# Two-branch mixer: the columns of w_in multiplied in pairs by seven half-size products

## What is computed

```
h = rmsnorm(x, g);  p = h @ w_in                       # 1024 x 9216
hc, b, c, z_a, q, k, v, z_r, g_a, g_r = split(p)
u = c * hc;  conv = w0*u[t-2] + w1*u[t-1] + w2*u[t]
a = ((b * conv) * silu(z_a)) @ w_a                     # 1024 x 1024
o, state = retention(rotary(q), rotary(k), v, state)   # 4 heads, chunks, per-head decay
r = (head_norm(o) * silu(z_r)) @ w_r                   # 1024 x 1024
x = x + (sigmoid(g_a) * a + sigmoid(g_r) * r) @ w_o    # 1024 x 1024
```

## Time and profile before

| | |
|---|---|
| time, median of 3 runs | 2542.15 us (2541.31 to 2542.98) |
| the profiled execution's span | 2539.6 us, 2.55 us under the median |
| PE busy | 2486.1 us of the span |
| POOL, DVE, ACT busy | 932.1, 857.9, 336.1 us |
| granted clock, mean | 0.991 |

### The profile page before, as it was taken

One profiled execution on the slowest core, in us unless ns is written; L12 is line 12 of the kernel. 1 busy time (PEld: TensorE's weight loads), 2 busy tenths in 40 slices (PEclk: granted clock), 3 DMA queues, 4 the chain that ended last, 5 costly groups with the idle time before them and its releaser, 6 DMA issues.

```text
span 2539.6 us, 35522 instructions
## 1 busy us (share of the span) xinstructions
PE 2486.1 (98%) x15141; PEld 2458.1 (97%) x15141; DVE 857.9 (34%) x805; ACT 336.1 (13%) x469; POOL 932.1 (37%) x426
## 2 busy tenths in 40 slices
PE   7999999999999999999989999999999999999998
PEld 6899999999999999999979999999999999999998
DVE  6552534331222222114384443523222222210153
ACT  5111121100010010001132111111000010000010
POOL 4333333343333333443362333333433333343442
PEclk8999999999999999999989999999999999999999
DMA  5111111111111111115311111111111111111162
GB/s 203 36 44 35 44 40 41 37 42 50 42 45 46 41 41 50 33 53 120 103 53 41 42 41 41 40 34 45 42 46 46 41 43 48 41 33 50 50 121 78
DMA packets 206120, 134.90 MB, mean 53 GB/s; under 512 B 12560, under 2 KB 197104, under 8 KB 204016
## 3 DMA queue, kind: packets, MB, share of 16 engines
q1 hardware_dynamic: 201312, 130.34, 17.9%
q10 hardware_dynamic: 4752, 3.75, 0.5%
HBM read 118.54 MB, written 15.53 MB: 53 GB/s over the span
## 4 chain that ended last, share of the span: by engine, by line
PE 84%; issue 6%; DVE 5%; POOL 2%; ACT 1%; DMA 0%; DVEq 0%; ACTq 0%; POOLq 0%; SPq 0%
PE ps L1044 80%; DVE x L786 1%; DVE act_lo L820 1%; POOL power L419 1%; POOL w_lo L410 1%; POOL w_hi L408 1%; DVE rstds L802 1%; PE ps L1117 1%; PE ps L1124 1%; PE ps L1090 1%; DVE T L764 0%; DVE V L804 0%; ACT row_squares L480 0%; DVE qT L766 0%; PE ps L1223 0%
## 5 line engine op out<-in xcount | busy, mean ns | idle before, releaser
L408 POOL TENSOR_TENSOR w_hi<-w_raw,zero 128x1024 fp32r<-128x1024 f32 x192 | 370.8, 1931 | 1420.0 <-PE ps L1044 1380.9
L1044 PE MATMUL ps<-act_hi,w_hi 128*128 128x364 f32 (+1 forms) x3840 | 858.9, 331 | 25.3 <-DVE act_lo L897 17.9
L1044 PE MATMUL ps<-act_lo,w_hi 128*128 128x364 f32 (+1 forms) x3840 | 848.3, 329 | 0.0
L1044 PE MATMUL ps<-act_hi,w_lo 128*128 128x364 f32 (+1 forms) x3840 | 844.1, 328 | 0.0
L1044 PEld LDWEIGHTS ps<-act_hi,w_hi 128*128 128x128 f32 x3840 | 661.8, 189 | 32.3 <-DVE act_lo L897 19.1
L1044 PEld LDWEIGHTS ps<-act_lo,w_hi 128*128 128x128 f32 x3840 | 666.6, 189 | 0.0
L1044 PEld LDWEIGHTS ps<-act_hi,w_lo 128*128 128x128 f32 x3840 | 665.8, 189 | 0.0
L410 POOL TENSOR_TENSOR w_lo<-w_raw,w_hi 128x1024 fp32r<-128x1024 f32 x192 | 512.5, 2669 | 15.1
L955 DVE TENSOR_TENSOR U<-ps,T 128x1092 f32<-128x1092 f32 x16 | 20.7, 1294 | 278.8 <-PE ps L1044 278.8
L924 DVE TENSOR_TENSOR U<-ps,T 128x728 f32<-128x728 f32 x16 | 14.7, 917 | 258.0 <-PE ps L1044 258.0
L1044 PE MATMUL ps<-o_hi,w_hi 128*128 128x364 f32 (+1 forms) x384 | 85.9, 332 | 5.9 <-DVE r L749 5.9
(11 more groups left out here) (179 smaller groups left out, 1748.2 us busy)
## 6 DMA issues: line engine op xcount, KB each, us to landing
w_raw<-in_w_in_dram SPq DMA_DIRECT2D x144, 512.0 KB, 3.6
x_keep<-x SPq DMA_DIRECT2D x8, 1092.0 KB, 8.4
x<-x_keep SPq DMA_DIRECT2D x8, 1092.0 KB, 7.3
w_raw<-in_w_r_dram SPq DMA_DIRECT2D x16, 512.0 KB, 3.9
w_raw<-in_w_a_dram SPq DMA_DIRECT2D x16, 512.0 KB, 4.6
w_raw<-in_w_o_dram SPq DMA_DIRECT2D x16, 512.0 KB, 4.0
x_rows<-in_x_prompt_dram SPq DMA_DIRECT2D x8, 512.0 KB, 7.0
out_dram<-y_rows SPq DMA_DIRECT2D x8, 512.0 KB, 3.3
```

Of the source, the lines that this page charges most:

```text
L408: nc.gpsimd.tensor_tensor(w_hi[s][:, :], w_raw[s][:, :], zero[:, 0:1].to_broadcast([P, D]), ALU.add).then_inc(weights_hi, 1)
L1044: done.append(mm(ps[:, 3 * s + c, 0:cn], w[:, a:a + P], b[:, k, c * THIRD:c * THIRD + cn], start=(k == 0 and t == 0), stop=(k == ktiles - ...
```

## The change

Two column tiles of w_in form a **pair** (`PAIRS`: HC with C, B with ZA, the two halves of a head's V and ZR, K with Q, GA with GR). A pair's product is a 2 x 2 block product: the weight's halves are its two column tiles by the two halves of k, the activation's are two halves of k by two halves of the columns (544). It is done by seven products of half size in k and in columns (M1 to M7; 4 k tiles x 3 terms x 2 parts of 272 columns) and sums of operands and results:

- POOL makes the sums of weights (sA, sB) and four low parts (`prepare_first`, `prepare_second`), ACT seven high parts (`high_w`), DVE three low parts (`low_w`).
- The sums of activations (T1 to T4) are made once per layer by POOL (`combine` in its block), from x tiles loaded back from DRAM and scaled by g (`scale_xs`), and split by ACT and DVE (`high_t`, `low_t`).
- The products add up in four PSUM regions; ACT copies four stages of them (`take`), and DVE adds regions and copies into result tiles E (its own `combine`).

The norm's factor no longer scales h: B11 to B22 are x times g, and DVE multiplies results by the factor `rs`. The first GA and GR tiles stay whole units (`gate_unit`, in four parts of 272 columns) and run while the sums T are made. Finished tiles (the convolution's product, v, z, k, q, gates, o, a) are stored to DRAM and loaded in the stage that uses them. All pairs come first; then each head runs beside two units of w_a (`row_tile`), then w_r with the merge, then w_o. Loops are written out.

```
+REGION = (0, 2, 4, 0, 4, 0, 6)
+FRESH = (True, True, True, False, False, False, True)
...
+            def low(l, n, j, src):
+                g = l * NP + n
+                pool.wait_ge(s_high, 7 * g + j + 1)
+                tt(s_lo[j][:, :, :], src, s_hi[j][:, :, :].bitcast(F32), ALU.subtract).then_inc(s_low_pool, 1)
...
+                tt(sA[:, :, :], quadrant(l, n, 1, 0), quadrant(l, n, 1, 1), ALU.add).then_inc(s_added, 1)
+                low(l, n, M1, quadrant(l, n, 0, 0))
+                pool.wait_ge(s_added, 4 * g + 1)
+                tt(sB[:, :, :], sA[:, :, :], quadrant(l, n, 0, 0), ALU.subtract).then_inc(s_added, 1)
+                low(l, n, M2, quadrant(l, n, 0, 1))
...
+            def take(l, n, i):
+                g = l * NP + n
+                act.wait_ge(product_done, 7 * g + (M1, M5, M6, M7)[i] + 1)
+                if g:
+                    act.wait_ge(combined, 4 * (g - 1) + (1, 3, 2, 4)[i])
...
+                do(parts(snap[i][:, :]), region((0, 4, 0, 0)[i]), ACT.Copy).then_inc(snapped, 1)
...
+            def gate_first(l, j):
+
+                dve.wait_ge(unit_done, l * NU + U_G + j + 1)
+                dve.wait_ge(rstd_copied, 2 * (l + 1))
...
+            def combine(l, n, q):
...
+                dve.wait_ge(product_done, 7 * g + (M2, M3, M7, M4)[q] + 1)
+                dve.wait_ge(snapped, 4 * g + (1, 3, 4, 4)[q])
...
+                    combine(l, n, 1)
+                    if more:
+                        low_w(l, n + 1, M3)
+                    combine(l, n, 2)
+                    if more:
+                        low_w(l, n + 1, M7)
+                    combine(l, n, 3)
+                    if more:
+                        low_w(l, n + 1, M4)
...
+            def product(l, n, j):
+
+                r, operand = REGION[j], (B11, B21, T1_, T2_, B22, T3_, T4_)[j]
+                for k in range(4):
+                    for t, (s, b) in enumerate(((s_hi, t_hi), (s_hi, t_lo), (s_lo, t_hi))):
+                        for p in range(2):
+                            i = mm(ps[:, r + p, 0:PART], s[j][:, k, :], b[operand][:, k, p * PART:(p + 1) * PART],
+                                   start=(FRESH[j] and k == 0 and t == 0), stop=(k == 3 and t == 2),
+                                   skip_group_check=True)
+                i.then_inc(product_done, 1)
...
+            def pair(l, n):
...
+                if g:
+                    pe.wait_ge(combined, 4 * g - 1)
+                    pe.wait_ge(snapped, 4 * g)
+                pe.wait_ge(s_low_pool, 4 * g + 1)
+                product(l, n, M1)
+                if n == 0:
+                    pe.wait_ge(g_scaled, 16 * l + 2)
+                pe.wait_ge(s_low_pool, 4 * g + 2)
+                product(l, n, M2)
...
+                if g:
+                    pe.wait_ge(combined, 4 * g)
+                product(l, n, M4)
...
+                        elif step == 3:
+                            turn_values(l, h, 0)
+                        elif step == 5 and h:
+                            turn_output_sample(hn - 1)
+                            turn_output(hn - 1, 0)
...
+                sp.wait_ge(o_stored, 32 * (HEADS - 1) * (l + 1))
+                sp.wait_ge(unit_done, l * NU + U_A + KT)
+                for k in range(6):
+                    if k == 4:
+                        sp.wait_ge(b_done, (l * HEADS + HEADS - 1) * NB + S_O + 1)
+                    sp.dma_start(o[k][2][:, :], kept["o"][k]).then_inc(o_loaded[k], 16)
```

More of the change, by code:

```diff
@@ L141, in build @@
[L141 to L151, removed]
@@ L156, in build @@
+        ident = place("ident", [P, P], F32)
+        ones = place("ones", [P, P], F32)
+        par = place("par", [P, NPAR], F32)
+        conv_keep = place("conv_keep", [P, 2, 2, KT], F32)
+        sums = place("sums", [P, 9], F32)
+        means = place("means", [P, 9], F32)
+        power = place("power", [P, 9], F32)
+        rstds = place("rstds", [P, 9], F32)
+        neg_half = place("neg_half", [P, 9], F32)
+        zero = place("zero", [P, 1], F32)
         assert at[0] <= nc.sbuf_usable_end - base, (at[0], nc.sbuf_usable_end - base)
@@ L163, in slot, with region, parts @@
             return ps[:, 3 * s:3 * s + 3, 0:THIRD]
[L165 to L174, removed]
+        def region(r):
+            return ps[:, r:r + 2, 0:PART]
+        def parts(a):
+            return a.rearrange("p (c n) -> p c n", n=PART)
@@ L445, in _ @@
[L445 to L457 removed]
+                tt(power[:, :], means[:, :], neg_half[:, :], ALU.pow).then_inc(norm_power, 1)
@@ new lines, in squares, with high_o, high_m @@
+            def squares(n, part, rows, c0, srcs):
+                act.wait_ge(o_squared, 3 * n + part)
+                for j, src in enumerate(srcs):
+                    i = do(junk[j][0:rows, :], src, ACT.Square, accum_out=sums[0:rows, c0 + j:c0 + j + 1])
+                i.then_inc(o_squared, 1)
+            def high_o(l, k):
+                act.wait_ge(o_loaded[k], 16 * (l + 1))
+                do(o[k][0][:, :], o[k][2][:, :], ACT.Copy).then_inc(o_high, 1)
+            def high_m(l, m):
+                act.wait_ge(merged_sum, l * KT + m + 1)
+                if m == KT // 2:
+                    act.wait_ge(states_stored, 32 * HEADS * (l + 1))
+                do(merged[m][0][:, :], gate_in[m % 2][:, :], ACT.Copy).then_inc(m_high, 1)
@@ new lines, in low_prod, with gate_a, mean @@
+            def low_prod(l, k):
+                dve.wait_ge(prod_high, l * KT + k + 1)
+                tt(prod[k][1][:, :], prod[k][2][:, :], prod[k][0][:, :].bitcast(F32), ALU.subtract).then_inc(prod_ready, 1)
+            def gate_a(l, m):
+                t = l * KT + m
+                dve.wait_ge(a_taken, t + 1)
+                dve.wait_ge(ga_loaded, 16 * (t + 1))
+                tt(a_out, a_out, X0, ALU.mult).then_inc(a_gated, 1)
+            def mean(hn, part, rows, c0, count):
+                h = hn % HEADS
+                dve.wait_ge(o_squared, 3 * hn + part + 1)
+                V_.tensor_scalar(means[0:rows, c0:c0 + count], sums[0:rows, c0:c0 + count], hc[0:rows, h, OA_:OA_ + 1],
+                                 EPS, ALU.mult, ALU.add).then_inc(o_mean, 1)
@@ new lines, in normalise @@
+            def normalise(hn, part, rows, c0, count, src):
+                h = hn % HEADS
+                dve.wait_ge(o_power, 3 * hn + part + 1)
+                d = done(V_.tensor_scalar(rstds[0:rows, c0:c0 + count], power[0:rows, c0:c0 + count], hc[0:rows, h, OB_:OB_ + 1],
+                                          None, ALU.mult))
+                after(d)
+                i = tt(V[h % 2][0:rows, c0:c0 + count, :], src, rstds[0:rows, c0:c0 + count, None].to_broadcast([rows, count, DV]), ALU.mult)
+                i.then_inc((c_free, a_free, b_free)[part], 1)
@@ new lines, in row_tile @@
+            def row_tile(u, slot_, k, tiles):
+                hi, lo = tiles[k][0], tiles[k][1]
+                for t, (w, b) in enumerate(((w_hi, hi), (w_hi, lo), (w_lo, hi))):
+                    for c, cn in enumerate((THIRD, THIRD, LAST)):
+                        i = mm(ps[:, 3 * slot_ + c, 0:cn], w[u % 2][:, k * P:(k + 1) * P], b[:, c * THIRD:c * THIRD + cn],
+                               start=(k == 0 and t == 0), stop=(k == KT - 1 and t == 2))
+                if k == KT - 1:
+                    i.then_inc(unit_done, 1)
```

1924 lines of the change are left out of this document (1118 added, 806 removed).

## The result

The changed kernel takes **2499.5 us** (median of 4 runs, 2498.5 to 2504.0) where the kernel before took 2542.6 beside it: a ratio of 0.9834, 95% interval 0.9822 to 0.9846. It is 43 us faster, 1.7%. The forecast was 2452, 90 us faster: the direction is right and the time lies in the range, but more than half of the gain that was forecast is missing.

What follows compares the result with a forecast made beforehand. PE, never idle at full clock, bounds the kernel; fewer columns gain, new waits lose. Layer 1 saves 48.3 us and layer 0 41.5: 2539.6 + 2.55 - 89.8 = 2452 us, range 2390 to 2520.

Steps and rivals of the forecast that it cites:

- The products: Pair loop on PE: 272-column matmuls take 126.8 ns (120.0 to 127.5), a pair 21.3 us against 23.84, 88.9 saved per layer.
- The edges: Between pairs, M1 waits for snap 3 and combine 2; the 68 later edges priced at nothing, 1.5 us to spare.
- The rival of the shared port: In the pairs, DVE waits for POOL's passes at each edge; slower than before from 2.8 us per edge; chance 0.10.
- the forecast's line for DVE: Price of DVE operations in the pairs: 0.14 us plus 1.07 ns per column.
- The start of a layer: Up to pair 0's end at S+60.8, where PE's own work is 33.5: 27.3 us of wait per layer.
- S: End of the broadcast at a layer's start: about 42.5 us in layer 0, 18.5 after w_o's last unit in layer 1.
- The heads: Heads beside two w_a units: 46.4 us per head with 3.5 of wait at turn_values, 185 per layer.
- w_r: Stage after the heads: o first lands at 8.5 us, PE's k0 at 11.2; 118 us with 20 of wait.
- Rival (3): Waits at layer start, conv_keep's stores and rstds were priced too large: 20 us per layer less, 2412; chance 0.14.
- The rival of slow retention: Late signals reach PE: each of eight heads waits 6 us more, w_r 10 per layer, 2520; chance 0.20.
- The tail: The kernel's end, 22.0 us from the last add, stays unchanged.

Runs made afterwards that it cites:

- e1: The four conv_keep stores moved from ahead of the loads of o into the pair loop, against the changed kernel: 2461.2 us, ratio 0.9683.
- e6: Changed kernel with conv_keep stores in the pair loop, gate_a behind K_lo, POOL's split behind normalise, gate_first(1) behind low_t(1): 2422.8 us, ratio 0.9534.

## Why the prediction was half right

**The products: right.** 5808 matmuls in 730.33 us are 125.7 ns each; 126.8 was forecast, 120.0 and 127.5 were the ends. A pair takes 21.1 us (forecast 21.3). The Trainium skill (TensorE: Matmul & The Clock Gate, Back-to-back issue gap) has a formula for the gap of an isolated matmul, which gives 115.8 ns for 272 columns; the trace of this stream differs and decides. **The edges: right.** No wait at the 68 later edges, as priced. The rival of the shared port costs nothing there, but its operations are long: DVE's products of 1024 and of 64 columns (L1075) take 1.75 and 1.31 us on average, where the forecast's line for DVE gives 1.24 and 0.21. Nothing on PE waits for them.

```profile
L1075 DVE SCALAR_TENSOR_TENSOR X<-U,par,X 128x1024 f32<-128x1024 f32 x32 | 56.0, 1751 | 13.8 <-ACT X L817 13.3
...
L1075 DVE SCALAR_TENSOR_TENSOR X<-U,par,X 128x64 f32<-128x64 f32 x32 | 41.9, 1310 | 0.0
```

**The start of a layer: too short, made good by luck.** With S at 41.16 (forecast 42.5), M1 starts at S+29.8 (27.1) and M2 at S+47.2 (40.5). The cheaper pairs make up for it, an error the other way that has nothing to do with this one. The passes of POOL that I took at 1.3 us for 544 columns take 1.33 to 1.37 with DVE idle and 1.7 to 1.85 beside DVE's low parts. The low parts, which I took at 0.72 each, suffer more: the last four before M2 take 6.87 us beside POOL, where four while POOL was idle took 2.61. What the rival of the shared port feared for the edges came true here, where the forecast had counted one wait for POOL.

```profile
58.58 2.61 DVE L1038 TENSOR_TENSOR t_lo<-t_raw,t_hi 128x544 fp32r<-128x544 f32 x4
...
80.12 6.87 DVE L1038 TENSOR_TENSOR t_lo<-t_raw,t_hi 128x544 fp32r<-128x544 f32 x4 [5.24 <-POOL t_raw L666]
```

**The heads: right in kind, 1.3 us short per period.** The wait at `turn_values` is 2.8 us where I had 3.5. What I left out: gate_a costs the pow 1 us, and the wait costs PE its clock, 0.9 us in the batch of turns alone.

**w_r: the step that failed.** "I place o's first landing at 8.5, high and low parts to 11.2, and PE's k0 there." PE's k0 came 21.0 and 25.3 us after the heads' end. I had sized the stores by how long SP's queue stood at them, 6.22 and 4.39 us. That is the time to issue them. Their landing is 13.8 to 26.9 us here, and the loads of o share the DMA engines with them. So the term of 118 us measured 135.7 and 140.1. Rival (3) had the stores short on an empty queue: the queue was short (2.4 us), the landing was not.

The price could have been read before the change. No view of the kernel before gives the landing of these stores, but its trace has the two loads of weights that SP issued right behind them (L302, at 1192.8 and 1200.6 us), and a window right behind the stores:

```profile
DMA to landing us min/median/max: 14.7/17.3/19.9
```

```profile
1192.00:1200.00 8.00, 8.00 (x50) 8.00 (x49) 2.71 (x2) 1.12 (x1) 3.82 (x2) 1.00 1.02 1
```

Loads that take 3.6 us in the median landed after 14.7 and 19.9, while the DMA engines were busy and moved 1 GB/s. PE worked all the while, so the cost did not show in the time.

With the stores moved away w_r takes what was forecast, and the kernel 2461, 9 us over the forecast: heads and tail. But this agreement of w_r is in part luck: k0 then comes 3.1 and 3.4 us after the heads' end, 8 us earlier than the forecast had it, and the first two units of layer 0 still end at 44.9 (forecast 45). Later waits for o and the clock, 0.64 in the window shown for e1, take what the early k0 gave. The rival of slow retention had this place (10 us more in w_r per layer), but for another reason, the serial chain of the last head; e1 shows that this chain did not make the 38 us that the moved stores won. With POOL's split out of its way as well, in e6, w_r loses another 6.4 and 3.1 us.

**The tail: 2.8 us, not counted.** The last norm sums on PE in two batches, before (L1024) and now (L1364). Before, the first ran as w_o ended; now it waits 1.45 us for x_end, and the second takes 3.31 us instead of 2.36, as the timeline of the changed kernel shows:

```profile
2473.53 2.15 PE L1364 MATMUL ps<-ones,acc 128*128 128x1 f32 x18 [1.45 <-DVE x_end L1313]
2475.61 3.31 PE L1364 MATMUL ps<-ones,sq 128*128 128x1 f32 x18
```

## What to carry to other kernels

What a transfer costs those behind it goes by its time to landing, and by that of the loads that already stand behind it, not by the time that the issuing queue stands at it; here stores of single elements belonged where PE does not wait for the next loads, and another queue did not help. Where a change takes away the work that covered a chain, price each short operation of that chain beside what the other engine does at that moment, and add the slower clock after a wait. Here the change won 43 us, and four small moves that its profile pointed to won another 77.

## What the runs showed of the hardware

A store of 1024 elements of 4 bytes (4 KB in all) takes 10.3 to 14.9 us to land, alone or first of two, when 544 KB take 3.6 to 8.5. Two such stores cost the loads behind them nearly as much as four (16.3 and 17.5 us at the least), one 10.4. After 2.8 us of idling eight transposes took 1.97 us at a granted clock of 0.50, after 1.2 us 1.09 at 1.00. Four DVE subtractions of 544 columns took 6.87 us beside POOL's passes and 2.61 while POOL was idle; a DVE operation of four columns took 1.86 us beside POOL's split and 0.23 without it.
